# Triangular inverses of a delta-rule recurrence: 32-token blocks in four array corners in place of 64-token ones in two

## The reference, cut to what matters

```python
def step(S, inp):
    r_t, w_t, k_t, v_t, kk_t, a_t = inp
    sa = jnp.einsum('bhvk,bhk->bhv', S, -kk_t)
    S = S * w_t[:, :, None, :] + sa[..., None] * (kk_t * a_t)[:, :, None, :] \
        + v_t[..., None] * k_t[:, :, None, :]
    return S, jnp.einsum('bhvk,bhk->bhv', S, r_t)
_, y = lax.scan(step, S0, (tm(r), tm(w), tm(k), tm(v), tm(kk), tm(a)))
```

## Time and profile before

| what | value |
|---|---|
| median of three runs | 3075.74 us (3074.43 to 3081.7) |
| the profiled execution, its own time | 3078.46 us |
| its span | 3076.6 us |
| mean granted TensorE clock | 0.971 |
| TensorE busy | 2841.3 us, 92% of the span |
| VectorE busy | 1365.9 us, 44% |
| ScalarE busy | 675.5 us, 22% |
| GpSimd busy | 937.3 us, 30% |

### The profile page before, as it was taken

One profiled execution on the slowest core, in us unless ns is written; L12 is line 12 of the kernel. 1 busy time (PEld: TensorE's weight loads), 2 busy tenths in 40 slices (PEclk: granted clock), 3 DMA queues, 4 the chain that ended last, 5 costly groups with the idle time before them and its releaser, 6 DMA issues. The chain is left out here.

```text
span 3076.6 us, 47029 instructions
## 1 busy us (share of the span) xinstructions
PE 2841.3 (92%) x19588; PEld 2245.5 (73%) x19588; DVE 1365.9 (44%) x1369; ACT 675.5 (22%) x954; POOL 937.3 (30%) x415
## 2 busy tenths in 40 slices
PE   6799999999999999999988899899998899898987
PEld 5677778888888888888776677776666676666775
DVE  8454442123522123123557443453363473444589
ACT  3233340010210000001323244411121121112231
POOL 3222214443444444344433111031111111112356
PEclk9899999999999999999999999999999999999998
DMA  3100001112111111111212000020100101002343
GB/s 119 33 28 28 20 21 48 48 48 97 47 48 48 48 52 47 51 48 48 68 71 79 23 14 20 8 74 18 46 30 32 40 32 36 32 32 91 96 157 103
DMA packets 40741, 156.02 MB, mean 51 GB/s; under 512 B 4640, under 2 KB 5152, under 8 KB 38944
## 3 DMA queue, kind: packets, MB, share of 16 engines
q1 hardware_dynamic: 31392, 110.21, 11.1%
q10 hardware_dynamic: 9216, 43.78, 3.8%
HBM read 133.00 MB, written 20.97 MB: 50 GB/s over the span
## 5 line engine op out<-in xcount | busy, mean ns | idle before, releaser
L2285 POOL TENSOR_TENSOR w_hi<-w_raw,one 128x1024 fp32r<-128x1024 f32 x200 | 389.7, 1948 | 2092.1 <-PE dps L283 1530.7
L283 PE MATMUL dps<-h_hi,w_hi 128*128 128x512 f32 x1904 | 610.0, 396 | 72.4 <-DVE sb_q L611 18.7
L283 PE MATMUL dps<-h_lo,w_hi 128*128 128x512 f32 x1904 | 603.1, 393 | 0.0
L283 PE MATMUL dps<-h_hi,w_lo 128*128 128x512 f32 x1904 | 601.4, 392 | 0.0
L2287 POOL TENSOR_TENSOR w_lo<-w_raw,w_hi 128x1024 fp32r<-128x1024 f32 x200 | 526.4, 2632 | 15.7
L283 PEld LDWEIGHTS dps<-h_hi,w_hi 128*128 128x128 f32 x1904 | 359.2, 190 | 161.5 <-issue 37.6
L283 PEld LDWEIGHTS dps<-h_lo,w_hi 128*128 128x128 f32 x1904 | 361.7, 190 | 76.1 <-issue 0.2
L283 PEld LDWEIGHTS dps<-h_hi,w_lo 128*128 128x128 f32 x1904 | 361.1, 190 | 76.5
L300 PE MATMUL dps<-h_lo,w_hi 128*128 128x512 f32 x352 | 132.7, 445 | 19.6 <-DVE rw_akt L1848 8.5
L300 PE MATMUL dps<-h_hi,w_lo 128*128 128x512 f32 x352 | 126.2, 428 | 18.7 <-DVE rw_akt L1860 8.8
L300 PE MATMUL dps<-h_hi,w_hi 128*128 128x512 f32 x352 | 128.5, 436 | 11.0 <-DVE rw_akt L1860 6.6
(11 more groups left out here) (346 smaller groups left out, 4158.6 us busy)
## 6 DMA issues: line engine op xcount, KB each, us to landing
w_raw<-w_stream SPq DMA_DIRECT2D x200, 512.0 KB, 3.6
x_again<-x_t ACTq DMA_DIRECT2D x2, 4096.0 KB, 14.4
gates<-gate_out ACTq DMA_DIRECT2D x16, 512.0 KB, 2.7
tmp<-gates ACTq DMA_DIRECT2D x16, 512.0 KB, 4.0
x_res<-x_t ACTq DMA_DIRECT2D x4, 1024.0 KB, 10.4
x_t<-x_res ACTq DMA_DIRECT2D x4, 1024.0 KB, 4.6
out_t<-x_again SPq DMA_DIRECT2D x16, 256.0 KB, 2.0
back<-branches ACTq DMA_DIRECT2D x7, 512.0 KB, 8.2
```

The costliest lines, as they stand in the source:

```text
L283: mm = k.nc.tensor.matmul(k.dps[0:rows, pair, h * HALF:(h + 1) * HALF], w[:, slot, sub + t, 0:rows], x(t)[:, h * HALF:(h + 1) * HALF], sta ...
L2285: g.tensor_tensor(k.w_hi[:, s], k.w_raw[:, s], ones, ALU.mult).then_inc(k.sem("w_hi_done"), 1)
```

## The change

The triangle is inverted in blocks of 32 tokens, four to a pair of heads and chunk, each on 32 partitions of its own. `xm`, `xb` (the transpose) and `t1` now have 32 columns for each chunk. Levels 1 to 4 make one 32x32 product for each block. Level 5 joins the two blocks of a head: t5 and xt5 are one 32x32 product for each head and chunk. ScalarE copies the diagonal blocks of the transposed inverse into the full `xt`, VectorE puts in the corner. lt and l are made 32 columns of output partitions at a time. The fills at a level go from 4 and 6 to 2 and 4, and before u0 there are as many as bring the count to 48. The core of the diff, without the constants' tables and the memory layout:

```diff
-FILL_MASKS, FILL_T, FILL_X, FILL_START, FILL_U, FILL_S, FILL_Y = 2, 4, 6, 4, 3, 5, 8
+FILL_MASKS, FILL_T, FILL_X, FILL_START, FILL_U, FILL_S, FILL_Y = 2, 2, 4, 4, 3, 5, 8
@@ rw_half_pe
+    def block_product(name, c, outs, lhs, rhs):
+        return k.nc.tensor.matmul(bank(k, name)[outs, c * CH:c * CH + rhs.shape[-1]], lhs, rhs, start=True, stop=True, skip_group_check=True)
+    def each_block(name, lhs, rhs):
+        for c in range(NC):
+            for q in QUARTERS:
+                mm = block_product(name, c, q, lhs[q, c, 0:BT], rhs[q, c, :])
+        mm.then_inc(product, 1)
+    def lower(name, lhs, rhs, off):
+        for c in range(NC):
+            for j in range(2):
+                for h, head in enumerate(HEADS):
+                    mm = block_product(name, c, QUARTERS[2 * h + j], lhs[head, c, j * BT:(j + 1) * BT],
+                                       rhs[head, c, j * BT:CH if off else (j + 1) * BT])
+        mm.then_inc(product, 1)
+    def corner(name, to, lhs, rhs):
+        for c in range(NC):
+            for h in range(2):
+                q = QUARTERS[2 * h + 1 - to]
+                mm = block_product(name, c, QUARTERS[2 * h + to], lhs(q, c), rhs[q, c, :])
+        mm.then_inc(product, 1)
-    each_chunk("lt", made["bq"], made["kkp"])
-    each_chunk("l", made["kkp"], made["bq"])
+    lower("lt", made["bq"], made["kkp"], True)
+    lower("l", made["kkp"], made["bq"], False)
@@ levels
-        each_chunk(f"t{l}", m["lt"], m["xm"])
+        if l < LEVELS:
+            each_block(f"t{l}", m["lt"], m["xm"])
+        else:
+            corner(f"t{l}", 1, lambda q, c: m["lt"][q, c, BT:CH], m["xm"])
...
-            each_chunk(f"x{l}", m["xt"], m["t1"])
-        each_chunk(f"xt{l}", m["t1"], m["xt"])
-    fill(FILL_T - 1)
+            each_block(f"x{l}", m["xb"], m["t1"])
+            each_block(f"xt{l}", m["t1"], m["xb"])
+        else:
+            corner(f"xt{l}", 0, lambda q, c: m["t1"][q, c, :], m["xb"])
+    fill(max(FILL_T, 6 * KT - filled) - 1)
...
-    u.wait(pe, COPIES, "akv")
+    u.wait(pe, COPIES, "diag")
@@ rw_dve
+    zeroed = v.memset(k.half["xt"][:, :, :], 0.0)
@@ rw_half_dve
-        mask("t1", f"t{l}", f"lev{l}").then_inc(made, 1)
+        if l < LEVELS:
+            mask("t1", f"t{l}", f"lev{l}").then_inc(made, 1)
+        else:
+            v.tensor_copy(m["t1"][:, :, :], taken(f"t{l}")[:, :, 0:BT]).then_inc(made, 1)
...
+        if l == LEVELS:
+            u.wait(dve, PRODUCTS, f"xt{l}")
+            for q in QUARTERS[::2]:
+                ins = v.tensor_scalar(m["xt"][q, :, BT:CH], taken(f"xt{l}")[q, :, 0:BT], -1.0, None, ALU.mult)
+            ins.then_inc(made, 1)
@@ rw_half_act
+    def diagonal():
+        u.wait(act, VALUES, f"xt{LEVELS - 1}")
+        for q, own in zip(QUARTERS, OWN):
+            ins = a.activation(m["xt"][q, :, own], m["xb"][q, :, :], ACT.Copy)
+        ins.then_inc(k.sem("rw_copy"), 1)
...
     if after is None:
+        diagonal()
         for n in (2, 3):
             rw_gate_act(k, act, u, n, gates)
...
         rw_exps_act(k, act, after)
+        diagonal()
     copy("u0")
     copy("w1_t")
```

More of the change, by code:

```diff
@@ L52 @@
 PI_BELOW = 3.1415925
+BT = 32
 CONST = {}
@@ L58 @@
                       ("sb_mask", P), ("mla_mask", P), ("mean_eps", P), ("pair_ident", HD), ("strict_t", HD),
-                      ("incl_t", HD), ("lev0", HD), ("lev0_t", HD), ("lev1", HD), ("lev2", HD), ("lev3", HD),
-                      ("lev4", HD), ("lev5", HD), ("rope_sum", P), ("pool_count", 64), ("reset", HALF),
+                      ("incl_t", HD), ("strict_b", HD), ("block_ident", BT), ("lev0", BT), ("lev0_t", BT), ("lev1", BT),
+                      ("lev2", BT), ("lev3", BT), ("lev4", BT), ("rope_sum", P), ("pool_count", 64), ("reset", HALF),
                       ("rope", 8)):
@@ L102, in __init__ @@
         self.nc, self.ctx, self.sems = nc, ctx, {}
-        self.ahead, self.half = {}, {}
+        self.ahead, self.half, self.x_room = {}, {}, 0
     def sem(self, name):
@@ L234, in layout @@
         at += 4 * kb
-    for name in ("lt", "akt", "xm", "xt", "t1", "arbt", "arkt", "kkp_tm", "v_tm", "be_tm", "ke_tm", "akv"):
+    for name in ("lt", "akt", "u0", "xt", "u", "arbt", "arkt", "kkp_tm", "v_tm", "be_tm", "ke_tm", "akv"):
         k.half[name] = k.at(f"rw_{name}", at, [NC, HD])
+        if name == "u0":
+            k.x_room = at
+        elif name == "u":
+            k.half["t1"] = k.at("rw_t1", at, [NC, BT])
         at += 2 * kb
     assert at <= V
-    for name, room in (("w1_t", "lt"), ("u0", "xm"), ("u", "t1"), ("s", "akt"), ("y", "akv")):
+    for n, name in enumerate(("xm", "xb")):
+        k.half[name] = k.at(f"rw_{name}", k.x_room + n * kb, [NC, BT])
+    for name, room in (("w1_t", "lt"), ("s", "akt"), ("y", "akv")):
         k.half[name] = k.half[room]
@@ L1419 @@
                + ["s_in"] + [f"{n}{c}" for c in range(NC) for n in ("u", "s")])
-COPIES = Steps("rw_copy", ["kkp_tm", "v_tm", "akv", "be_tm", "ke_tm", "u0", "w1_t"])
+COPIES = Steps("rw_copy", ["kkp_tm", "v_tm", "akv", "be_tm", "ke_tm", "diag", "u0", "w1_t"])
 Y_PRODUCTS = Steps("rw_y_product", ["y", "mean", "var"])
@@ L1426 @@
 TAKEN_BY = {"rk": (VALUES, "rkv"), "lt": (VALUES, "xt_part"), "l": (VALUES, "x_part"), **{n: (VALUES, n) for n in ["ak_t", "rb_t", "rk_t"] + LEVEL_NAMES},
-            **{n: (COPIES, n) for n in COPIES.names}}
+            **{n: (COPIES, n) for n in COPIES.names if n != "diag"}}
 RW_BLOCKS = 8
@@ L1475, in masked @@
 def masked(k, name):
-    return const(k, name).rearrange("p (a b) -> p a b", a=1).to_broadcast([P, NC, HD])
+    part = const(k, name).rearrange("p (a b) -> p a b", a=1)
+    return part.to_broadcast([P, NC, part.shape[2]])
 def both(k, out, lhs, rhs, start=True, stop=True):
@@ L1484, in both @@
     return mm
+QUARTERS = tuple(slice(q * BT, (q + 1) * BT) for q in range(P // BT))
+OWN = tuple(slice(q % 2 * BT, (q % 2 + 1) * BT) for q in range(P // BT))
 def rw_pe(k, pe):
@@ L1808, in mask @@
     def mask(out, name, which):
-        return v.tensor_tensor(m[out][:, :, :], taken(name), masked(k, which), ALU.mult)
+        return v.tensor_tensor(m[out][:, :, :], taken(name)[:, :, 0:m[out].shape[2]], masked(k, which), ALU.mult)
     u.wait(dve, PRODUCTS, "rk")
@@ L1814, in rw_half_dve @@
     u.wait(dve, PRODUCTS, "lt")
-    mask("lt", "lt", "strict_t").then_inc(made, 1)
-    for first, which, out, part in (("lt", "lev0_t", "xt", "xt_part"), ("l", "lev0", "xm", "x_part")):
+    mask("lt", "lt", "strict_b").then_inc(made, 1)
+    for first, which, out, part in (("lt", "lev0_t", "xb", "xt_part"), ("l", "lev0", "xm", "x_part")):
         u.wait(dve, PRODUCTS, first)
@@ L1819, in rw_half_dve @@
         u.wait(dve, VALUES, part)
-        v.tensor_tensor(m[out][:, :, :], masked(k, "pair_ident"), m[out][:, :, :], ALU.subtract).then_inc(made, 1)
+        v.tensor_tensor(m[out][:, :, :], masked(k, "block_ident"), m[out][:, :, :], ALU.subtract).then_inc(made, 1)
     result_step()
@@ L1827, in rw_half_dve @@
         u.wait(dve, PRODUCTS, f"t{l}")
-        mask("t1", f"t{l}", f"lev{l}").then_inc(made, 1)
+        if l < LEVELS:
+            mask("t1", f"t{l}", f"lev{l}").then_inc(made, 1)
+        else:
+            v.tensor_copy(m["t1"][:, :, :], taken(f"t{l}")[:, :, 0:BT]).then_inc(made, 1)
         result_step()
-        for n, out in (("x", "xm"), ("xt", "xt")):
-            if (n, l) != ("x", LEVELS):
+        for n, out in (("x", "xm"), ("xt", "xb")):
+            if l < LEVELS:
                 u.wait(dve, PRODUCTS, f"{n}{l}")
-                v.tensor_tensor(m[out][:, :, :], m[out][:, :, :], taken(f"{n}{l}"), ALU.subtract).then_inc(made, 1)
+                v.tensor_tensor(m[out][:, :, :], m[out][:, :, :], taken(f"{n}{l}")[:, :, 0:BT], ALU.subtract).then_inc(made, 1)
+        if l == LEVELS:
[3 more added lines that the diff above has]
+            ins.then_inc(made, 1)
         result_step()
@@ L2384, in constants @@
     put("incl_t", r <= f)
-    for n in range(6):
+    put("strict_b", np.where(f < BT, r % BT < f, r < BT))
+    r, f = p % BT, np.arange(BT)[None, :]
+    put("block_ident", r == f)
+    for n in range(5):
         b = 1 << n
```

## The result

| | before | after |
|---|---|---|
| median of four runs | 3075.09 us (3073.61 to 3081.7) | 3111.97 us (3106.29 to 3114.58) |
| ratio, 95% interval | | 1.0113 (1.0093 to 1.0134) |
| span of the profiled execution | 3076.6 us | 3109.7 us |
| mean granted TensorE clock | 0.971 | 0.960 |

The kernel became 37 us slower; 28 us faster was forecast. The forecast's sign is wrong, and that is not a matter of noise: no run of after is as short as any run of before.

A forecast was written before the change was run, and what follows sets the result against it. TensorE was taken as the bound, busy 2841.3 of 3076.6 us. Savings of 3 x 2.2 + 4.2 + 4 x 4.4 = 28 us off the 3075.7 median gave 3048, range 3030 to 3120 (the forecast's own 3034 to 3062).

The forecast's parts named there:

- Pace of a 32x32 product: Levels 1 to 4: 64 passes in four corners take 0.58 us, saving 0.35 a product, 4.2 us a half.
- Work taken off TensorE: Recurrent stage: small products take 5.3 us less TensorE work in each half, 42 us over eight halves.
- 4.2 + 0.9 + 0.3: TensorE savings a half in us: products of levels 1 to 4, then level 5's t5 and xt5, then the masks.
- the 0.1 a level: Between t and x, the mask path takes 1.0 us against 0.95 of TensorE cover, so 0.1 us of waiting.
- The step that failed: Small products: measured paces fit corner streaming, none shows a hand-out limit, so 0.58 us a product was taken.
- Rival 1: Handing out instructions is the limit at all 14 doubled products, deciding from 15.5 ns a pass: 3121 us; chance 0.33.
- Fills: None removed, 6 a level in place of 10; their own time is the same wherever they stand, but they cover less.
- the wait in front of `s_in`: First halves: 2.25 us idle there, put 0.6 us less because four more fills stand ahead of it.
- VectorE's lateness in levels: First halves of pairs 1 to 3: VectorE's queue ends late, 6.0 us idle against 2.3 now, 3.7 more.
- ScalarE: the copies: Four diagonal copies, 1.2 us; hidden in first halves, 0.5 us idle before w1_t in second halves, up to 2.
- The clock (rival 3): New idle times in first-half levels bring spells at 1.2 GHz, 7 to 27 us: 3055 to 3075 us; chance 0.10.

The follow-up runs named there:

- `after_burst`: The changed kernel with the t product of level 1 made eight times in a row; 3208.43 us (one run).
- `after_old_fills`: The changed kernel with the old fills (4 and 6 a level) and gate copy 2 ahead of the diagonal copies on ScalarE; 3055.99 us, ratio 0.9941.
- `before_new_fills`: The kernel before with only the fills of the change (2 and 4 a level, 48 before u0); 3094.83 us, ratio 1.0063.
- `after_half_blocks`: The changed kernel with the 32x32 products of levels 1 to 4 made for chunks 0 to 3 alone; 3022.38 us (one run).
- `transpose_new_fills`: The changed kernel, gate copy 2 first, VectorE transposes replacing xt products at levels 1 to 4, fills 2 and 4; 3042.03 us, ratio 0.9892.
- experiment 5: The changed kernel with only gate copy 2 moved ahead of the diagonal copies on ScalarE; 3108.98 us, ratio 1.0109.
- `after_gate_order`: The run of experiment 5: the changed kernel with only gate copy 2 ahead of the diagonal copies; 3108.98 us, ratio 1.0109.

## Why the prediction was wrong

**Pace of a 32x32 product: right.** 0.58 us were taken. A product's record of 0.75 us holds the 0.2 of the last pass's latency, so 64 passes take 0.55; the 128 passes of `after_burst` take 1.27 less 0.2, 8.4 ns each. So the 25 ns floor of "TensorE: Matmul & The Clock Gate" (the Trainium skill, section "Wait — 56ns, not 53.3ns?") can stand at most for one corner: over four corners it does not hold here. Its part 3, which lets matmuls in different corners start some 4 ns apart, is nearer, and was rightly preferred; in this trace the starts of the four corners are 6 to 8 ns apart.

**Work taken off TensorE: right.** Stage of `after_old_fills`, 20.3 us shorter than before's, with 28.4 us more idle time in gaps over 0.15 us: some 45 us of work went (with about 4 more for 10 us less of low clock), 5.6 a half against 5.3 forecast. In second halves, a level without holes took 3.8 us (t at 2394.41, the next at 2398.18), as said. Two slips of the sum are small: 4.2 + 0.9 + 0.3 is 5.4 and not 5.3, and four fills with two changes are by its own prices (0.22, and 0.34 for two changes) 1.2 us and not 0.95, so the 0.1 a level was no wait. In after, 1.12 us lie between the end of t's last record and x (2298.35 to 2299.47).

**The step that failed** is the sentence "every measured pace fits the streaming time of a corner and none shows a limit of the hand-out". It priced each product by itself, and 64 passes alone do run at corner speed. What is limited is a stretch of products. Four levels of the second half of pair 1 take from 2394.41 to 2417.68, 23.3 us, for 4 x 396 instructions: 14.7 ns each, of which the corners and fills need 9.8. At the rate of `after_burst` (13.6) it would be 21.5. So the levels now run at the supply's rate, not at TensorE's. The kernel before could have warned, though not given the price: its page has the instruction queue, 115 packets and 1.88 MB, 16 KB each, and a level of 396 instructions asks for a packet every 2.5 us, where of its 114 distances between packets 113 are over 4.9 us and the shortest is 3.5. A rate that lay beyond all rows was taken as free. Rival 1 had the right direction and one right row ("no instruction rate above one in 14.6 ns"), but by another mechanism, a floor under each pass (15.5 ns and more), which would show as long products and not as fast ones with holes.

The Trainium skill has this machine in "Runtime: NRT & Kernel Launch", section "Instruction fetch mechanics": instructions are refilled in blocks of 256 while the current block is executed, and this is mostly hidden because the sequencer dispatches more slowly than the blocks are filled. The block size agrees with this trace. The second half does not: TensorE takes an instruction of these products every 4.2 ns, so 256 last 1.1 us, and the next 256 run 3.5 us after the start of the last.

**Fills: put too low, and at `s_in` wrong in sign.** Moving them costs 20 us in the kernel before. "Their own time is the same wherever they stand, but they cover less" was counted in the levels alone, and the wait in front of `s_in` was put 0.6 less a half. It grew from 2.25 to 4.12 us, 8 us in all. VectorE there, in after (answers to the last rows):

```profile
2328.50 1.22 DVE L1738 TENSOR_TENSOR rw_z<-dps,inv 128x1024 f32<-128x1024 f32 x1 [1.41 <-PE dps L307]
2329.84 1.14 DVE L1804 TENSOR_TENSOR rw_rp<-rw_r,rw_t 128x512 f32<-128x512 f32 x1
2330.91 2.84 DVE L1804 TENSOR_TENSOR rw_kkp<-rw_kk,rw_t 128x512 f32<-128x512 f32 x1
2333.67 0.68 DVE L1804 TENSOR_TENSOR rw_bq<-rw_b,rw_t 128x512 f32<-128x512 f32 x1
...
2335.48 0.18 DVE L1902 COPY rw_akt<-rw_s 128x64 f32<-128x64 f32 x1
```

VectorE takes out z before it gets to `s_in`, and z's 48th fill now comes last of all, right ahead of u0; VectorE waits 1.41 us for it. The end of z also sets GpSimd free, and its pair of weight operations meets VectorE's multiplications:

```profile
2328.54 1.89 POOL L2347 TENSOR_TENSOR w_hi<-w_raw,one 128x1024 fp32r<-128x1024 f32 x1 [42.57 <-PE dps L307]
2330.51 2.69 POOL L2349 TENSOR_TENSOR w_lo<-w_raw,w_hi 128x1024 fp32r<-128x1024 f32 x1
```

The kkp multiplication takes 2.84 instead of 0.68 us beside it. The error: a fill is not only cover, it is a product that somebody waits for. Who takes the tile out, and what becomes free with it, had to be followed. In the kernel before none of the seven kkp multiplications took over 0.69 us; in after and in `before_new_fills` most of them take 2.84. (That GpSimd's work is what stretches VectorE's was seen where the two meet and not tried by itself.)

**VectorE's lateness in levels: put about twice too high.** 6.0 us a first half were forecast; in after, waits for the masks of t add up to 2.1 us in five places, which fits that the holes give VectorE the time that it lacked. The two versions with the new fills and next to no holes have 11.6 us of them in all (`after_half_blocks`, where the products cover less) and 8.1 (`transpose_new_fills`), against 19.7 forecast for the four first halves and 7.3 before. So the term was too large, if they are a measure of it, and that is not what broke the forecast.

**ScalarE: the copies cost little, the last half was missed.** Four diagonal copies take 1.69 us (1.2 forecast). Waits for w1_t stand in the whole run once with 6.3 us, in the last half, and once with 1.1; experiment 5 shows that the order of copies gives 1.1 us at this wait and nothing clear in the time. The 6.3 are mostly the fills': `before_new_fills`, which has no diagonal copies, has 5.2 at the same place. There the last gate tile is finished late, and in the last half ScalarE issues eight DMAs (3.6 and 0.45 us) between its copy and that of u0.

**The clock (rival 3): true as a companion.** Time at the lower clock in the stage went from 64.9 us in nine spells to 136.5 in nineteen. What it costs is estimated from two versions that differ in it and in their fills: `after_gate_order` has 95.6 us more of it than `after_old_fills` (150.2 against 54.6), a stage 55.0 us longer, and 17.3 us more idle time; the other 38 us are put down to the slower work, 0.4 us for each us. By this the 71.6 us more in after are some 28 us. The spells of pair 1's first half begin behind the hole of 2.14 us (at 2307.88), behind the wait of 0.99 for VectorE's copy of t5 (at 2324.94) and in the wait for `s_in` (at 2335.18), as those of the earlier trace rows did around idle time; `after_half_blocks`, without holes, is at 71.7 us.

**The sum as it came out**, in the stage: 45 us less work, 46 us more idle time (holes 42, `s_in` 8, w1_t 7, and 11 less elsewhere, half of it waits for the masks of t), some 28 us more from the clock: +29, measured +30.2. Nothing of the 42 was in the forecast's sum, and the clock stood in a rival only. The terms of work and clock are estimates and lean on each other; the idle times are read. The medians say the same another way: products and order alone -18, fills alone +20, both +37. The 35 us over the sum of the two are what low fills do in a kernel that is short of instructions: longer holes and more than twice the time at low clock (136.5 us against 54.6).

What stays open: what starts a packet. In the burst one starts 1.1 us after the last one's instructions began to run, also where those ran at the lower clock and took 1.7 us; whether TensorE could be made to ask for it sooner was not tried.

## What to carry to other kernels

Splitting a product into smaller ones for more array corners gains on each product and loses on the stream: count instructions over the few us that a stretch of small products lasts (two for each float32 pass, fills too) and hold them against what the instruction queue delivers, here one in 13.6 ns, before counting what the corners need. Where the stream is too dense, take products away from TensorE (here a transpose that VectorE does for the price of the subtraction that it replaces) rather than put fills between; and when fills move, follow the tiles that they finish to whoever takes them out.

## What the runs showed of the hardware that was not expected

- TensorE's instructions come in packets of 256, and starving it gives whole holes of about 2.2 us rather than a slower pace: 3.47 us for 256 instructions in `after_burst`, against 1.1 us in which they run.
- Four corners take a 32-column float32 pass every 8.4 ns, load included, two corners a 64-column one every 29 ns. A 16-column pass behind a 64-column load took 58 ns a corner at the full clock, as long as a 64-column pass, and 107 at the lower: the reading that fits is that the load was the limit.
- A transpose of the 32x32 blocks of a 128x256 float32 tile takes VectorE 0.45 us, a subtraction of that size 0.42.
